# Three inner layer norms worked in halves of the tokens, with the first weight panel of the next stage run half by half

## The reference, cut to what matters

```python
x = layer_norm(ALPHA * x + mix, ln1_g[l], ln1_b[l])     # mix = token_mixing(x, ...), with w_in and w_o
ffn = conv_ffn(x, ffn_w_up[l], ffn_conv_w[l], ffn_conv_b[l], ffn_w_down[l])
x = layer_norm(ALPHA * x + ffn, ln2_g[l], ln2_b[l])
```

## Time and profile before

| | us |
|---|---|
| median of 3 runs (3949.2, 3952.55, 3953.59) | 3952.55 |
| profiled execution, its own time | 3953.41 |
| span of the profiled execution, first to last instruction | 3951.6 |
| PE busy in the span | 3690.2 (93%) |
| DVE busy | 2085.7 (53%) |
| ACT busy | 1442.3 (36%) |
| POOL busy | 645.3 (16%) |
| mean granted clock of TensorE, as a share of full speed | 0.96 |

### The profile page before, as it was taken

The page is one execution under the profiler, slowest core; times in us unless marked ns, Lnnn a source line. Parts: engine busy times, 40 slices in busy tenths (PEclk is TensorE's granted clock), DMA queues, the critical chain, the costliest instruction groups (busy, mean ns, idle before and its releaser), DMA issues.

```text
span 3951.6 us, 50824 instructions
## 1 busy us (share of the span) xinstructions
PE 3690.2 (93%) x19794; PEld 2974.2 (75%) x19794; DVE 2085.7 (53%) x3730; ACT 1442.3 (36%) x2248; POOL 645.3 (16%) x651
## 2 busy tenths in 40 slices
PE   8889999999988999999999887999999979899999
PEld 6676677787766766777878765788888879777887
DVE  4646755766456366656664535355454252564333
ACT  3445643443133446424331325331112233552222
POOL 1110121212220011122122110113333122000000
PEclk9989999999989899999999897999999989999999
DMA  4111232323331111333233100112322111212222
GB/s 155 60 64 49 86 114 105 121 108 133 112 113 61 54 59 65 118 123 125 104 135 129 66 22 1 43 70 80 118 91 101 65 54 54 70 49 75 101 96 80
DMA packets 65808, 339.01 MB, mean 86 GB/s; under 512 B 6816, under 2 KB 8352, under 8 KB 39968
## 3 DMA queue, kind: packets, MB, share of 16 engines
q1 hardware_dynamic: 65568, 335.78, 23.6%
HBM read 327.36 MB, written 8.39 MB: 85 GB/s over the span
## 4 chain that ended last, share of the span: by engine, by line
PE 76%; DVE 13%; ACT 8%; issue 2%; POOL 1%; DMA 0%; DVEq 0%; ACTq 0%; POOLq 0%; SPq 0%
PE ps L1718 23%; PE ps L1720 22%; PE ps L1719 22%; DVE wl L1969 3%; PE ps L1707 3%; PE ps L1845 2%; ACT wh L1864 2%; PE ps L1727 2%; DVE tt L1977 1%; PE ps L1838 1%; DVE pb L2195 1%; DVE acc L1977 1%; DVE hl L1977 1%; ACT opb L1957 1%; DVE u L1969 1%
## 5 line engine op out<-in xcount | busy, mean ns | idle before, releaser
L1969 DVE TENSOR_TENSOR wl<-raw,wh 128x2048 fp32r<-128x2048 f32 (+2 forms) x275 | 554.9, 2018 | 402.9 <-ACT wh L1864 383.2
L1864 ACT ACTIVATE wh<-raw 128x2048 fp32r<-128x2048 f32 (+2 forms) x275 | 457.2, 1663 | 815.7 <-PE ps L1720 811.4
L1718 PE MATMUL ps<-hh,wh 128*128 128x512 f32 (+1 forms) x1248 | 449.3, 360 | 11.0 <-DVE hl L1977 9.4
L2218 POOL TENSOR_TENSOR lt<-lt,cs 128x1024 f32<-128x1024 f32 x96 | 188.2, 1960 | 1657.6 <-DVE acc L1977 1657.6
L1719 PE MATMUL ps<-hl,wh 128*128 128x512 f32 (+1 forms) x1248 | 444.8, 356 | 0.0
L1720 PE MATMUL ps<-hh,wl 128*128 128x512 f32 (+1 forms) x1248 | 444.8, 356 | 0.0
L1718 PE MATMUL ps<-xhb,wh 128*128 128x512 f32 x832 | 371.4, 446 | 13.6 <-DVE xlb L1969 10.9
L1719 PE MATMUL ps<-xlb,wh 128*128 128x512 f32 x832 | 338.2, 406 | 0.0
L1720 PE MATMUL ps<-xhb,wl 128*128 128x512 f32 x832 | 338.0, 406 | 0.0
L1718 PE MATMUL ps<-xha,wh 128*128 128x512 f32 x704 | 284.1, 404 | 14.6 <-DVE wl L1969 12.0
L1719 PE MATMUL ps<-xla,wh 128*128 128x512 f32 x704 | 281.6, 400 | 0.0
(11 more groups left out here) (264 smaller groups left out, 7323.3 us busy)
## 6 DMA issues: line engine op xcount, KB each, us to landing
raw<-in_wts SPq DMA_DIRECT2D x199, 1024.0 KB, 4.8
lt<-in_wts SPq DMA_DIRECT2D x110, 512.0 KB, 3.5
raw<-in_wts SPq DMA_DIRECT2D x44, 512.0 KB, 3.4
raw<-in_wts SPq DMA_DIRECT2D x28, 448.0 KB, 3.1
x_scratch<-xt SPq DMA_DIRECT2D x3, 2048.0 KB, 9.1
xt<-x_scratch SPq DMA_DIRECT2D x3, 2048.0 KB, 8.1
oe<-in_relb SPq DMA_DIRECT2D x16, 384.0 KB, 3.9
bt<-in_big SPq DMA_DIRECT2D x1, 2688.0 KB, 9.5
```

The source lines that it names most:

```text
L1718: T.matmul(u.out, u.sh, u.mh, start=u.first, stop=False)
L1864: A.activation(u.h, u.raw, ACT.Copy).then_inc(*act.inc())
L1969: V.tensor_tensor(o_, a, b, op).then_inc(*dve.inc())
L2218: G.tensor_tensor(o_, a, b, op).then_inc(*pool.inc())
```

## The change

Everything concerns the three inner norms (`not last2`) and the start of the stage after each.

- ACT scales only token tiles 0 to 2 right after their statistics; tile 3 is scaled later, in the middle of the first half's work.
- The turns, the shift and the split work on halves of 256 tokens: half 0 (token tiles 0 and 1) for all eight chunks, then half 1. One bank holds two chunks of a half. The shift (gain and bias, from the bank to `tz`) goes to DVE for chunks 0, 1, 4, 5, 6, 7 (`ln_shift`, a tensor_scalar) and to ACT for chunks 2 and 3 (`ln_shift_act`). ACT makes the high part from `tz`, no longer from the bank, and DVE the low part (`ln_halves`).
- The first panel of the next stage runs `first_halves`: for half 0 the 16 `dense` steps of 256 tokens, and between them the turns, shifts and splits of half 1; then the 16 steps for half 1.
- The last panel of the norm's matmul is given back (`p.done`) only after half 0, so the `wh` copy of the next stage's second panel stands behind half 0 on ACT, and its `wl` behind half 0 and ahead of half 1 on DVE.
- The fences at the start of `mix` and `ffn1` are gone (all four uses, so 4 one-column instructions fewer on ACT, DVE and POOL each). `ln_gain` starts after 20 steps, where it was 6.

```diff
+        def first_halves(p, xh, xl):
+            j, joint[0] = joint[0], None
+            bs = banks[4:6]
+            for y in range(2):
+                n0, n1 = y * 256, y * 256 + 256
+                for k in range(8):
+                    for m, b in enumerate(bs):
+                        b.w = dense(b.ap[:, n0:n1], p.h[:, k, m * P:m * P + P], p.l[:, k, m * P:m * P + P], xh[:, k, n0:n1], xl[:, k, n0:n1],
+                                    k == 0, k == 7, k == 7, [j[y][k]], *((p.w, b.free) if y == k == 0 else ()))
+                        step()
+                    if y == 0 and k in (2, 4, 6, 7):
+                        j[2]((2, 4, 6, 7).index(k))
+            p.done(b.w)
+            return [[b] for b in bs]
...
-            fw = fence(stores=False)
+            fw = now()
...
+                    if (half, q) == (1, len(pieces) - 1):
+                        last = p, t
+                    else:
+                        p.done(t)
...
-                        z_t[i] = ACT_(add("ln_scale", x=XT[:, i, :], rs=RS[:, i, :]))
+                        z_t[i] = DVE(add("ln_stats", rs=RS[:, i, :]))
+                        if i < 3 or last2:
+                            scaled(i)
...
+                def turn_half(y, g):
+                    b = banks[g]
+                    for k in (2 * g, 2 * g + 1):
+                        for i in (2 * y, 2 * y + 1):
+                            b.w = PE(add("ln_turn", out=b.ap[:, (2 * (k % 2) + i % 2) * P:(2 * (k % 2) + i % 2) * P + P], x=XT[:, i, k * P:k * P + P],
+                                         eye=ident, came=z_t[i], less=int(k < 4), free=b.free + [tab], end=(k, i) == (2 * g + 1, 2 * y + 1)))
+                def shift(y, k):
+                    b, j = banks[k // 2], k // 2 % 2 * 256
+                    u = add("ln_shift_act" if k // 2 == 1 else "ln_shift", t=TZ[k % 2][:, j:j + 256], b=b.ap[:, k % 2 * 256:k % 2 * 256 + 256],
+                            bias=gb[:, 8 + k:9 + k], scale=gb[:, k:k + 1], came=b.w, t_free=tt_free[k % 4])
...
+                def halves(y, k):
+                    j, n0, n1 = k // 2 % 2 * 256, y * 256, y * 256 + 256
+                    u = add("ln_halves", t=TZ[k % 2][:, j:j + 256], h=XH[:, k, n0:n1], l=XL[:, k, n0:n1], came=shifted[k])
...
+                def second_half(g):
+                    turn_half(1, g)
+                    for k in (2 * g, 2 * g + 1):
+                        shift(1, k)
+                        if k:
+                            halves(1, k - 1)
+                    if g == 3:
+                        halves(1, 7)
...
+                for g in range(4):
+                    turn_half(0, g)
+                for k in range(8):
+                    shift(0, k)
+                    if k:
+                        halves(0, k - 1)
+                    if k == 2:
+                        scaled(3)
+                halves(0, 7)
+                last[0].done(last[1])
+                joint[0] = marks[0], marks[1], second_half
...
+                    later(small, 20 + 5 * i, gain)
...
-                    later(small, 6 + 5 * i, gain)
...
-            w = fence(stores=False)
+            w = now("pe", "act", "dve")
...
+                elif kind == "ln_shift":
...
+                    ts(u.t, u.b, u.scale, u.bias, ALU.mult, ALU.add)
```

More of the change, by code:

```diff
@@ L607, in fm_pair @@
             return bs, b.w
+        joint = [None]
+        def first_halves(p, xh, xl):
[12 more added lines that the diff above has]
+            return [[b] for b in bs]
         def both_chunks(p, nk, xh, xl, ns, ring, per_k, first):
+            if first and joint[0]:
+                yield from first_halves(p, xh, xl)
+                return
             if first:
@@ L657, in build @@
         x_ready = x_ks[7]
+        x_last = [x_ready]
         cs_t = evac(CS[:, :, :].rearrange("p k n -> p (k n)"), Q("cs"), [prm], ACT.Silu)
@@ L713, in mix @@
             GG = buf(f"gg{l}", [P, S], z0 + 18184)[:, :]
-            fw = fence(stores=False)
+            fw = now()
             ada_ring[0] = GR
             tmp, t1 = GS
-            xw = [x_ready]
+            xw = x_last
             s_lam = sem(f"s_lam{l}")
@@ L1093, in layer_norm, with scaled @@
             z_t = [None] * 4
+            def scaled(i):
+                z_t[i] = ACT_(add("ln_scale", x=XT[:, i, :], rs=RS[:, i, :], came=z_t[i]))
             for half in range(2):
@@ L1105, in layer_norm @@
                         bs[i].w = t
-                    p.done(t)
+                    if (half, q) == (1, len(pieces) - 1):
+                        last = p, t
+                    else:
+                        p.done(t)
                     if piece_done and half:
@@ L1113, in layer_norm, with gain @@
                     if half:
-                        z_t[i] = ACT_(add("ln_scale", x=XT[:, i, :], rs=RS[:, i, :]))
+                        z_t[i] = DVE(add("ln_stats", rs=RS[:, i, :]))
+                        if i < 3 or last2:
+                            scaled(i)
             XH, XL = (XHa, XLa) if which == 1 else (XHb, XLb)
             gb = Q(("lnp", l, which))
+            tt_free, shifted = [[], [], [], []], [None] * 8
+            if not last2:
+                marks = [[None] * 8, [None] * 8]
+                def turn_half(y, g):
[8 more added lines that the diff above has]
+                            bias=gb[:, 8 + k:9 + k], scale=gb[:, k:k + 1], came=b.w, t_free=tt_free[k % 4])
+                    shifted[k] = ACT_(u) if k // 2 == 1 else DVE(u)
+                    b.free = [shifted[k]]
+                def halves(y, k):
+                    j, n0, n1 = k // 2 % 2 * 256, y * 256, y * 256 + 256
+                    u = add("ln_halves", t=TZ[k % 2][:, j:j + 256], h=XH[:, k, n0:n1], l=XL[:, k, n0:n1], came=shifted[k])
+                    marks[y][k] = x_ks[k] = DVE(u)
+                    tt_free[k % 4] = [DVE(u)]
+                def second_half(g):
[6 more added lines that the diff above has]
+                        halves(1, 7)
+                        x_last[0] = x_ks[7]
+                for g in range(4):
[9 more added lines that the diff above has]
+                joint[0] = marks[0], marks[1], second_half
+                pg, pb_ = get((("lng", which), l), 1), get((("lnb", which), l), 1)
+                for i in range(4):
+                    def gain(i=i):
+                        u = add("ln_gain", x=XT[:, i, :], g=pg.v[:, 0, :], b=pb_.v[:, 0, :], g_t=pg.w, b_t=pb_.w, came=banks[3].w)
+                        if i == 3:
+                            pg.done(DVE(u))
+                            pb_.done(POOL(u))
+                            add("load", dst=xkeep.rearrange("(i p) n -> p i n", p=P), src=XT[:, :, :], sem=s_xd, free=[POOL(u)])
+                            nxd[0] += 1
+                            stored[0] = (s_xd, 16 * nxd[0])
+                    later(small, 20 + 5 * i, gain)
+                return
@@ L1123, in layer_norm @@
                                              came=z_t[i], less=int(k0 == 0), free=banks[k].free + [tab] if i == 0 else [], end=i == 3))
-            tt_free = [[], []]
             for k in range(8):
                 b = banks[k]
[L1127 to L1134, removed]
+                u = add("ln_last", x=XX[:, k, :], b=b.ap, bias=gb[:, 8 + k:9 + k], scale=gb[:, k:k + 1], came=turned_t[k])
+                x_ks[k] = ACT_(u)
                 b.free = [ACT_(u)]
-                if last2:
-                    early["sums"](k, x_ks[k])
+                early["sums"](k, x_ks[k])
+            last[0].done(last[1])
             x_ready = x_ks[7]
[L1139 to L1149, removed]
-                    later(small, 6 + 5 * i, gain)
         def ffn1(l):
@@ L1907, in act_program @@
                 elif kind == "ln_scale":
-                    act.wait_ge(*at(DVE(u)))
+                    act.wait_ge(*at(u.came))
                     for half in range(2):
@@ L1917, in act_program @@
                     A.activation(u.x, u.b, ACT.Identity, bias=u.bias, scale=u.scale).then_inc(*act.inc())
-                elif kind == "ln_split":
+                elif kind == "ln_shift_act":
                     act.wait_ge(*at(u.came))
@@ L1924, in act_program @@
                     A.activation(u.t, u.b, ACT.Identity, bias=u.bias, scale=u.scale).then_inc(*act.inc())
+                elif kind == "ln_halves":
+                    act.wait_ge(*at(u.came))
                     act.wait_ge(*act.own())
-                    A.activation(u.h, u.b, ACT.Identity, bias=u.bias, scale=u.scale).then_inc(*act.inc())
+                    A.activation(u.h, u.t, ACT.Copy).then_inc(*act.inc())
                 elif kind == "up_conv":
@@ L2110, in dve_program @@
                     V.bn_stats(u.stats, u.x).then_inc(*dve.inc())
-                elif kind == "ln_scale":
+                elif kind == "ln_stats":
                     dve.wait_ge(*dve.own())
@@ L2116, in dve_program @@
                     stt(u.rs[:, 14:15], u.rs[:, 12:13], -1.0, u.rs[:, 15:16], ALU.mult, ALU.mult)
```

(8 more changed lines are left out.)

## The result

The changed kernel takes 3962.05 us, the median of 9 runs, and the kernel before 3949.25 (9 runs on the same chip): ratio 1.0032, 95% interval 1.0022 to 1.0042. It is slower by 12.8 us, 0.32%, where the prediction took 0.2% as what can be told from no change. Forecast were 3958.7 us with a range of 3949.5 to 3966, in which the time lies, and, as likeliest, a time within 0.2% of the kernel before, which it is not.

What follows compares the result with a forecast made beforehand. PE, busy 93%, was taken to wait for DVE's list behind the norms. Adding 1.18, 3.76 and 1.18, in all 6.1 us, to the profiled 3953.41 gave 3959.5, less 0.9 for the median 3958.7 us; range 3949.5 to 3966.

Steps and rivals of the forecast that it cites:

- DVE's list decides: After the inner norms, PE waits for DVE's work, 7.1 us for a `wl` and 9.7 for a `gs`.
- the first gain is the landmark: On DVE behind each norm: from first `xt` gain to third panel 18.52 us, unchanged; only its start moves.
- The sum over the norms, 6.1 us: Statistics' end to first gain at the inner norms: +1.18 us at first and third, +3.76 at second.
- The shift: DVE's tensor_scalar out of a bank in the norms: 0.48 us taken, bounds 0.352 and 0.54.
- the early first panel: Next stage's first panel on PE: first matmul 6.5 us earlier, only lengthening the later wait, so no gain.
- Rival 3: First panel's early start after each norm counts in full: 19.5 us faster, 3933 us; chance 0.06.
- Rival 4: PE's clock stays at the lower level through the second panel: up to 3968.3 us; chance 0.04.
- The allowance of 1.5 us for the moved attention steps: Mixing of layer 1: reordered attention steps may move the time by 1.5 us either way.
- "Which no edit moves": End of the norms' statistics, the starting point of the count: taken as unchanged, 680.78 us at norm 1.
- The profiled execution against the median: Whole kernel: median of the runs taken 0.9 us below the profiled execution's 3953.41.
- "Within 0.2%": Whole kernel: time within 0.2% (7.9 us) of the kernel before, counted as same; chance 0.68.
- rival 2: Every DVE instruction in the norms dearer, shift 0.54, gap 0.15: +12.1 us, 3964.6 us; chance 0.24.

Runs made afterwards that it cites:

- e2: Kernel before with its background-work counter moved on by 8 at the mixing of layer 1, giving the change's order there: 3956.45 us, ratio 1.0015.
- e12: Kernel before with its background-work counter moved on by 4 at the mixing of layer 1, a third order: 3942.08 us, ratio 0.9981.
- e8: Changed kernel with every shift of the inner norms on ScalarE, VectorE only subtracting: 3951.51 us, ratio 0.9994.
- e11: Kernel before without the fence at the start of each mixing: 3951.31 us, ratio 1.0006.
- e1: Changed kernel with 16 instead of 32 background-driving steps in the first panel: 3954.19 us, ratio 1.0012.

## Why the prediction was right or wrong

- **DVE's list decides and the first gain is the landmark: right.** 18.54 us behind it at norm 1 and 11.99 us to PE's rope matmul at norm 2 are those of before (18.52 and 11.99).
- **The sum over the norms, 6.1 us: right in kind, small by 0.9.** `wl` ended at 14.16 us, as computed. The shift is the mis-sized term: 0.544 us, my upper bound, where I took 0.48. The four behind subtraction 2 in each half make 0.5 us a norm, but half 0's share is hidden, since DVE waits there for `wh`, which ACT ended on time (DVE's wait was 1.28 us, 1.4 computed). Half 1's share is 0.26 us; so first gains at 23.14 at norms 2 and 3 instead of 22.94. Norm 1's 23.42 has 0.28 more, which arose ahead of subtraction 1 of half 1, where DVE waited 0.82 us for ACT and at norm 3 only 0.54. The subtraction (0.425), ACT's pieces (0.417, 0.563) and the gaps of 0.10 came out as priced.
- **Costed at nothing, the early first panel: right.** PE started 1.9 us after the statistics (1.7 forecast) and waited 6.2 us at the third panel. Rival 3 didn't happen. Rival 4 neither: PE's granted clock in the second panel was 1.00 (702.0 to 712.9 us).
- **The allowance of 1.5 us for the moved attention steps: this is the step that failed.** I read it from two mixings that are alike in length (652.90 and 649.90 us), which showed the result of two orders and not what an order can do. It was 5.8 us in this profile; by the ratios the change's order cost 5.9 us in e2 and the third order won 7.5 in e12. The norms' 7.0 us alone would have stayed within the 7.9 us of the 0.2%. The 5.8 us are no fixed price of the order, though, since e8 had it too and ran at 0.9994.
- **"Which no edit moves", the end of the statistics: not so in the profiles.** It came at 677.59 us at norm 1 instead of 680.78. The missing fence explains at most a part (e11 lies in between), and e11's total is no shorter.
- **The profiled execution against the median.** I took 0.9 us between them from three runs; over nine it was 4.2, so the difference of the medians (12.8) is larger than that of the profiles (10.1). That the time came within 3.4 us of the forecast is therefore luck in part: the kernel before was taken 3.3 us too slow, and the difference itself, forecast at 6.1 us, was twice that.
- **The classes.** "Within 0.2%" had 0.68 and the result, 0.32%, is over that bound, inside the range. The time is the one rival 2 names, but its mechanism gave only part: the shift at 0.54 yes, the gap of 0.15 no.

Open: which wait in the attention's steps lets PE's clock fall. The order alone does not fix it, since e8 had the change's order and its `mix1` took 661 us, and e11 the old order and 669; what came before in time matters as well, and each profile shows one execution. What makes `ffn0` 0.7 us longer in the change is open as well.

## What to carry to other kernels

Splitting a step in halves to start the next engine early pays only if that engine is what the following stage waits for; find the landmark where two lists meet, and price the longer list. Whatever changes a counter that places background work changes the program far from the edit: compare the orders there, hold the counter fixed to see the edit by itself, and try the counter's other values, which here were worth more than the change. Before moving work back out of a stall, ask which buffer it holds.

## What the runs showed of the hardware

A 128x256 float32 tensor_scalar out of a bank with two per-partition scalars takes 0.544 us, against 0.352 for the shortest of that width inside SBUF; the same affine step on ScalarE takes 0.563, so it gains nothing by going to VectorE. The mean granted clock of a run, 0.957 to 0.965 in the kernels whose gains stay in place, orders its time, some 1.5 to 2.6 us for each thousandth in the kernel before (three series) and 1.8 in e1, by fitted lines.
